# Four output units, two norms and four units behind them, in halves of 256 tokens

## The chip, the cores and the metric

The kernel runs on one core of one Trainium2 chip. The metric is the device time of one execution in microseconds (us), as the median of several. Engines are called as in the profile: PE (TensorE), ACT (ScalarE), DVE (VectorE), POOL (GpSimd), SP (SyncE, which here only issues DMAs).

## The reference

Two transformer blocks follow each other on 512 tokens of width 1024. The change lies at the end of the second block, between its attention and its second feed-forward net, whose first matmuls it also touches:

```python
y = g_na * (o_na.reshape(B, T, -1) @ w_o_na) + g_mla * (o_mla.reshape(B, T, -1) @ w_o_mla)
y = y @ w_out                                       # the second output projection
x = _residual(x, y, g[3], m[5], 1.0)                # x + gate * rmsnorm(y) * gain
h = _modnorm(x, g[4], m[6], m[7])                   # rmsnorm(x) * gain * (1 + scale) + shift
x = _residual(x, _swiglu(h, ffn2_w1, ffn2_w3, ffn2_w2), g[5], m[8], HALF_STEP)
```

Both norms go over the 1024 features of a token, so each waits for the whole row of its input.

## The kernel before, in words

Activations lie transposed: partition = feature, X has 8 tiles of 128 features x 512 tokens. Every matrix is cut into **units** of 1024 x 128 (512 KB) that stream through four slots. A unit's way is always the same: SP's DMA into RAW (`refill`, L433) once `units_done` says that the slot's last unit is through; ACT rounds it to the high part WHI (`convert`, L553); POOL writes the low part WLO = RAW - WHI (`lows`, L455, four instructions of 256 columns), **in the place of RAW**; PE multiplies. Three products (high x low, high x high, low x high) make one exact fp32 product, so a unit on 512 tokens is 24 matmuls. A slot is free for its next DMA only when the last matmul of the unit that it holds has run. All orders are written out by hand, one program for each engine with semaphores.

The stretch of interest, on each engine:

- **PE.** The eight units of the projection, `w_out2` (0 and 1 as a pair, then one after the other, L2343 and L2347, banks m % 4). Then 9 idle matmuls (`spin`, L2424; an fp32 matmul leaves two records), which only keep the engine at work, the ones-matmul that sums the squares of y over the features (`sum_of`, L2433), 14 more idle ones, eight ones-matmuls for the squares of X (L3231), 15 idle ones. Then the four first units of the net, `ffn2` + 0 to 3: 0 and 1 as a `pair`, tile by tile as the normed input arrives (L2368, L2369, L2373), 2 and 3 each whole. Their last matmuls are far apart in time: units 0 and 1 first, 2 then, 3 last. Then `net`: `first_down` (L2853), which multiplies by units `ffn2` + 4 and 5 and needs the weights of + 4, both halves of the gated product (`_l`), and then `seven` for each pair of units.
- **DVE.** For each unit of the projection it copies the product to YO (L2247) and adds ACT's square to the sum (L1376). `post` (L1796 to L1802) scales the eight tiles by the norm's factor and gain, adding the odd ones to X; POOL adds the even ones (`even_tiles`, L469). Then it scales X tile by tile into PSUM (L2264) and writes the low parts HLO (L2258). Three sums for the net follow (L2269 to L2272), `rest_of_sums` with the low parts TLO (L1886), and the copies of `first_down`'s products to Y (L1866) ahead of the first pair's sums (L1941).
- **ACT.** `project` rounds a unit and squares a tile of YO, turn about; `factor` makes Ln and Exp of the sum (L584, L588); L1298 squares X; L1302 and L1303 write HHI and HRAW. `net` begins with `convert` of `ffn2` + 3, the SiLU (L1061), `convert` of + 4 and of + 5, the round of the gated product (L1064) and three rounds THI (L1014).
- **POOL.** `lows` through `ffn2` + 2, the even tiles, then `lows` of + 3, 4 and 5.

Of the kernel before, what the change touches and what calls it, by code (L numbers as in the profile page):

```python
# [22 lines left out]
ALU = mybir.AluOpType  # L23
# [87 lines left out]
for _name, _n in _vec:  # L111
# [43 lines left out]
def build(nc, t):  # L155
    with ExitStack() as ctx:
# [83 lines left out]
        (SQ2, RS2, TN2), _ = region(r_at, ("SQ2", [P, 2, N2], F32), ("RS2", [P, N2], F32), ("TN2", [P, 2, N2], F32))  # L240
# [48 lines left out]
        (YO,), _ = region(g_at, ("YO", [P, KD, S], F32))  # L289
# [157 lines left out]
        def _(pool):  # L447
# [94 lines left out]
        def _(act):  # L542
# [749 lines left out]
            project("yo", "w_out2", "p3", SQ2, YO)  # L1292
            factor("p3", 6)
            for k in range(KD):
                act.wait_ge(*tile_at("p3", k))
                if k >= 2:
                    act.wait_ge(*norm_at("a4", "ms", k - 1))
                nc.scalar.activation(SQ2[:, k % 2, 0:S], X[:, k], ACT.Square).then_inc(s("norm_sq"), 1)  # L1298
            factor("a4", 4, n=KD)
            for k in range(KD):  # L1300
                act.wait_ge(*norm_at("a4", "t", k + 1))
                nc.scalar.activation(HHI[:, k, 0:S], ps[:, (5, 7)[k % 2]], ACT.Identity, bias=mod[:, 6 * KD + k, 0:1]).then_inc(s("norm_hi"), 1)  # L1302
                nc.scalar.activation(HRAW[:, k, 0:S], ps[:, (5, 7)[k % 2]], ACT.Identity, bias=mod[:, 6 * KD + k, 0:1]).then_inc(of_strassen("raw"), 1)  # L1303
# [30 lines left out]
        def _(dve):  # L1334
# [909 lines left out]
            clear(TN2[:, 1, 0:S])  # L2244
            for m in range(KD):
                wait_unit(UNIT["w_out2"] + m)
                V.tensor_copy(YO[:, m], ps[:, m % 4]).then_inc(s("yo"), 1)  # L2247
                add_square("p3", TN2[:, 1, 0:S], SQ2, m, m)
            dve.wait_ge(s("yo"), KD + 4)
            post("p3", lambda k: YO[:, k], cf(6), (5, 7), lambda j: TN2[:, j % 2, 0:S])  # L2250
            dve.wait_ge(*norm_at("p3", "x", KD // 2))
            dve.wait_ge(*norm_at("p3", "px", KD // 2))
            z = NETS[1]

            def last_low(k):
# [73 lines left out]
        def _(pe):  # L2329
# [811 lines left out]
            def latent_values(b):  # L3141
# [8 lines left out]
                mm.then_inc(*((s("mv_ready"), 1) if b < 5 else (units_done, 1)))  # L3150
# [78 lines left out]
            for k in range(KD):  # L3229
# [198 lines left out]
```

## Time and profile before

| | |
|---|---|
| median of 3 runs | 2281.15 us (2280.82 to 2284.95) |
| the profiled execution | 2280.16 us, its span 2278.3 us |
| granted PE clock over the span | 0.998 |
| PE busy | 2218.7 us, 97% |
| the projection's last unit is through; idle matmuls begin | 1892.8 us |
| first matmul of `ffn2` | 1912.05 us |
| first matmul of `first_down` | 1935.58 us |

Times of rows are us from the span's start. A matmul's printed duration is longer than the distance to the next one, since they are pipelined; what a stretch costs is read from starts. "<-" names what ended an idle time.

### The profile page before, as it was taken

What the parts mean: (1) busy time and instruction counts of PE and PEld (TensorE: products, weight loads), DVE (VectorE), ACT (ScalarE), POOL (GpSimd) and SP (SyncE); (2) the same over time, 40 slices, a digit from 0 to 9 for tenths busy, and PEclk for the clock granted to TensorE, in tenths of its full rate; (3) what the DMA queues carried; (4) which work ended last, traced back from release to release, by engine and by line L of the source; (5) the groups of instructions that cost most, each with busy time, mean ns of one, the idle gap of its engine ahead of it and who ended that gap; (6) DMA issues with size and microseconds to landing.
All of it is one profiled execution on the core that took longest, in us unless ns stands there. A gap on an engine that the chain in (4) does not pass through costs nothing.

```text
span 2278.3 us, 34847 instructions
## 1 busy us (share of the span) xinstructions
PE 2218.7 (97%) x12540; PEld 1920.9 (84%) x12540; DVE 1312.9 (58%) x2104; ACT 959.0 (42%) x1490; POOL 1296.7 (57%) x1440
## 2 busy tenths in 40 slices
PE   7999999999999999999999999999989999999997
PEld 6778787678888879999999989877777887999997
DVE  4525632598878778454554655234247546877666
ACT  3354644444233454332332343255546535444443
POOL 3434465199988766554644634333346164887775
PEclk9999999999999999999999999999999999999999
DMA  4322142355555542222212222222230021333232
GB/s 157 104 81 84 56 133 90 111 175 198 198 188 199 186 148 74 66 65 74 75 58 73 75 74 72 75 88 81 67 105 29 20 102 60 98 101 104 95 110 75
DMA packets 67952, 229.27 MB, mean 101 GB/s; under 512 B 7264, under 2 KB 12640, under 8 KB 67680
## 3 DMA queue, kind: packets, MB, share of 16 engines
q1 hardware_dynamic: 50944, 176.67, 23.1%
q10 hardware_dynamic: 16864, 50.60, 6.7%
q8 instruction: 100, 1.64, 0.3%
q14 instruction: 44, 0.36, 0.1%
HBM read 224.36 MB, written 2.10 MB: 99 GB/s over the span
## 4 chain that ended last, share of the span: by engine, by line
PE 81%; DVE 8%; issue 5%; ACT 3%; POOL 3%; DMA 0%; ACTq 0%; POOLq 0%; DVEq 0%; SPq 0%
PE ps L2343 19%; PE ps L2853 11%; PE ps L2347 10%; PE ps L2912 7%; PE ps L2908 7%; PE ps L2909 7%; PE ps L3062 4%; PE ps L2399 3%; POOL WLO L455 2%; PE ps L2354 1%; PE ps L3004 1%; PE ps L3182 1%; PE ps L3033 1%; PE ps L3047 1%; PE ps L3200 1%
## 5 line engine op out<-in xcount | busy, mean ns | idle before, releaser
L455 POOL TENSOR_TENSOR WLO<-RAW,WHI 128x256 fp32r<-128x256 f32 x996 | 865.2, 904 | 708.6 <-ACT WHI L553 708.0
L553 ACT ACTIVATE WHI<-RAW 128x1024 fp32r<-128x1024 f32 x249 | 260.6, 1056 | 275.2 <-DMA RAW<-in_stream_dram 266.6
L474 POOL TENSOR_TENSOR WLO<-RAW,WHI 128x256 fp32r<-128x256 f32 x240 | 235.5, 1002 | 196.4 <-DVE SRAW L1941 77.7
L2343 PE MATMUL ps<-HLO,WHI 128*128 128x512 f32 (+2 forms) x848 | 306.6, 378 | 0.0
L2343 PE MATMUL ps<-HHI,WHI 128*128 128x512 f32 (+2 forms) x848 | 300.5, 371 | 0.0
L2347 PE MATMUL ps<-HHI,WLO 128*128 128x512 f32 (+2 forms) x848 | 192.5, 371 | 0.3 <-POOL WLO L455 0.3
L2343 PEld LDWEIGHTS ps<-HLO,WHI 128*128 128x128 f32 (+1 forms) x848 | 154.7, 188 | 32.4 <-issue 4.3
L2343 PEld LDWEIGHTS ps<-HHI,WHI 128*128 128x128 f32 (+1 forms) x848 | 154.9, 188 | 30.4 <-issue 2.6
L2347 PEld LDWEIGHTS ps<-HHI,WLO 128*128 128x128 f32 (+1 forms) x848 | 149.3, 188 | 28.3 <-POOL WLO L455 0.5
L2853 PE MATMUL ps<-GLO,WHI 128*128 128x384 f32 (+1 forms) x480 | 143.7, 353 | 1.3 <-POOL WLO L455 1.1
L2853 PE MATMUL ps<-GHI,WHI 128*128 128x384 f32 (+1 forms) x480 | 143.5, 353 | 0.0
L2853 PE MATMUL ps<-GHI,WLO 128*128 128x384 f32 (+1 forms) x480 | 143.5, 352 | 0.0
L2908 PE MATMUL ps<-HLO,WHI 128*128 128x384 f32 (+1 forms) x480 | 140.3, 308 | 0.0
L2909 PE MATMUL ps<-HHI,WHI 128*128 128x384 f32 (+1 forms) x480 | 140.3, 308 | 0.0
L1644 DVE SCALAR_TENSOR_TENSOR ADA<-ADA,CB 128x1024 f32<-128x1024 f32 x72 | 107.6, 1495 | 7.6 <-DVE DOT L1644 2.3
L1869 DVE TENSOR_TENSOR Y<-Y,ps 128x768 f32<-128x768 f32 (+1 forms) x72 | 58.9, 818 | 88.5 <-PE ps L2853 88.0
L1644 DVE SCALAR_TENSOR_TENSOR DOT<-ADA,CB 128x1024 f32<-128x1024 f32 x72 | 105.1, 1459 | 5.5 <-issue 5.1
L1031 ACT ACTIVATE SHI<-SRAW 128x512 fp32r<-128x512 f32 x120 | 75.7, 631 | 73.2 <-DVE SRAW L1956 53.8
L1026 ACT ACTIVATE WHI<-RAW 128x1024 fp32r<-128x1024 f32 x80 | 63.8, 838 | 89.9 <-DMA RAW<-in_stream_dram 89.9
L2853 PEld LDWEIGHTS ps<-GLO,WHI 128*128 128x128 f32 x480 | 87.7, 188 | 8.2 <-POOL WLO L455 1.6
L2909 PE MATMUL ps<-THI,SHI 128*128 128x384 f32 (+1 forms) x320 | 93.6, 308 | 0.0
L2908 PE MATMUL ps<-TLO,SHI 128*128 128x384 f32 (+1 forms) x320 | 93.6, 308 | 0.0
(508 smaller groups left out, 5333.9 us busy)
## 6 DMA issues: line engine op xcount, KB each, us to landing
RAW<-in_stream_dram SPq DMA_DIRECT2D x329, 512.0 KB, 3.3
ADA<-in_ada_dram ACTq DMA_DIRECT2D x72, 512.0 KB, 4.0
BM<-in_bias_dram ACTq DMA_DIRECT2D x8, 448.0 KB, 3.9
DECAY<-in_decay_dram ACTq DMA_DIRECT2D x4, 512.0 KB, 3.7
C<-in_ctx_dram ACTq DMA_DIRECT2D x2, 1024.0 KB, 5.5
out_dram<-X SPq DMA_DIRECT2D x16, 128.0 KB, 1.8
X<-in_x_dram SPq DMA_DIRECT2D x2, 512.0 KB, 5.9
X<-in_x_dram ACTq DMA_DIRECT2D x2, 512.0 KB, 6.9
```

The lines of the kernel that those rows point to most:

```text
L455: op = nc.gpsimd.tensor_tensor(WLO[:, slot(u), k:k + 2], RAW[:, slot(u), k:k + 2], WHI[:, slot(u), k:k + 2].bitcast(F32), ALU.subtract)
L474: op = nc.gpsimd.tensor_tensor(WLO[:, j, k:k + 2], RAW[:, j, k:k + 2], WHI[:, j, k:k + 2].bitcast(F32), ALU.subtract)
L553: nc.scalar.activation(WHI[:, j], RAW[:, j], ACT.Copy).then_inc(unit_hi, 1)
L1031: nc.scalar.activation(out, x, ACT.Copy).then_inc(of_strassen("hi"), 1)
L1644: V.scalar_tensor_tensor(out, w, 1.0, CB[:, v], ALU.mult, ALU.mult, accum_out=mod[:, bass.ds(4 * i + a0, 1), v]).then_inc(s("ada_used"), 1)
L2343: nc.tensor.matmul(out, high[k], x[:, k, tok], start=(k == 0 and n == 0), stop=False)
L2347: mm = nc.tensor.matmul(out, low[k], hi[:, k, tok], start=False, stop=(k == kt - 1))
L2853: mm = nc.tensor.matmul(ps[:, bank, 0:n], w[:, j, k0 + k], x[:, k, n0:n0 + n], start=(first and k == ks[0] and i == 0), stop=(final and k ...
L2908: nc.tensor.matmul(product(z, p, n), high[:, k], x_lo[:, k], start=(k == 0 and not more), stop=False, skip_group_check=more)
L2909: nc.tensor.matmul(product(z, p, n), high[:, k], x_hi[:, k], start=False, stop=False, skip_group_check=more)
L2912: mm = nc.tensor.matmul(product(z, p, n), low[:, k], x_hi[:, k], start=False, stop=(k == 3), skip_group_check=more)
L3062: mm = nc.tensor.matmul(ps[:, 7], w, x[:, k, x_tok], start=(k == 0 and n == 0), stop=(k == KD - 1 and n == 2))
```

## The change

The projection's units 4 to 7, both norms and units `ffn2` + 0 to 3 work on 256 tokens at a time, and the norms' element work takes two tiles (2 x 256) in one instruction. The first half of the tokens is normed while PE does the second half of the projection. ACT takes over the copy to YO and puts the gain on it; the gain of the second norm also goes to ACT's bias instruction, so DVE multiplies by the factor alone, into SBUF. All idle matmuls here are gone. The order on PE, ACT and DVE, and on POOL, in the diff's own lines (helpers of one line each, semaphore tables and buffer addresses left out):

```diff
 # PE
-            for m in range(2, KD):
+            for m in range(2, 4):
+                unit(UNIT["w_out2"] + m, 0, [(ps[:, m], x_tok)], hi=HHI, lo=HLO)
...
+            def half_tiles(first, last, h):
+                for b in range(first, last):
+                    wait_weights(UNIT["ffn2"] + b)
+                for j in range(4):
+                    pe.wait_ge(*norm_at("w2", "hi", 8 * h + 2 * j + 2))
+                    for k in (2 * j, 2 * j + 1):
+                        for b in range(first, last):
+                            u, out = slot(UNIT["ffn2"] + b), ps[:, 2 * b, half_of(h)]
+                            nc.tensor.matmul(out, WHI[:, u, k], HHI[:, k, half_of(h)], start=(k == 0), stop=False)
+                            nc.tensor.matmul(out, WLO[:, u, k], HHI[:, k, half_of(h)], start=False, stop=False)
+                    pe.wait_ge(*norm_at("w2", "lo", 4 * h + j + 1))
+                    for b in range(first, last):
+                        for k in (2 * j, 2 * j + 1):
+                            mm = nc.tensor.matmul(ps[:, 2 * b, half_of(h)], WHI[:, slot(UNIT["ffn2"] + b), k], HLO[:, k, half_of(h)],
+                                                  start=False, stop=(k == KD - 1))
+                        if h and j == 3:
+                            mm.then_inc(units_done, 1)
+            for m in range(4, KD):
                 pe.wait_ge(s("yo"), m + 1)
-                unit(UNIT["w_out2"] + m, 0, [(ps[:, m % 4], x_tok)], hi=HHI, lo=HLO)
-            sum_of("p3", TN2[:, 1, 0:S], 6, wait=9, idle=4)
-            spin(4, 14)
-
-            for k in range(KD):
-                pe.wait_ge(*norm_at("a4", "sq", k + 1))
-                nc.tensor.matmul(ps[:, 4], const[:, ONES], SQ2[:, k % 2, 0:S], start=(k == 0), stop=(k == KD - 1)).then_inc(s("norm_ms"), 1)
-            spin(1, 15)
+                out_half(m, 0).then_inc(s("part_ready"), 1)
+            out_half(4, 1)
+            p3_total(0)
+            for m in range(5, KD):
+                out_half(m, 1)
+            a4_total(0)
+            p3_total(1)
+            pe.wait_ge(s("yo"), 16)
+            half_tiles(0, 2, 0)
+            half_tiles(2, 4, 0)
+            a4_total(1)
+            half_tiles(0, 4, 1)
...
-            u = UNIT["ffn2"]
-            pair(u, 0, [[(ps[:, 0], x_tok)], [(ps[:, 2], x_tok)]], HHI, HLO, lambda k: (norm_at("a4", "hi", k + 1), norm_at("a4", "lo", k + 1)))
-            unit(u + 2, 0, [(ps[:, 4], x_tok)], hi=HHI, lo=HLO)
-            unit(u + 3, 0, [(ps[:, 6], x_tok)], hi=HHI, lo=HLO)
 # ACT
+            def out_rows(m, h=None):
...
+                nc.scalar.activation(SQ2[:, m % 2, cols], x, ACT.Square).then_inc(s("norm_sq"), 1)
+                nc.scalar.activation(YO[:, m, cols], x, ACT.Identity, scale=coef[:, 6, m:m + 1]).then_inc(s("yo"), 1)
+            def modulated(h, j):
+                act.wait_ge(*norm_at("w2", "t", 4 * h + j + 1))
+                for b in range(2):
+                    k = 2 * j + b
+                    for dst, landed in ((HHI, s("norm_hi")), (HRAW, of_strassen("raw"))):
+                        nc.scalar.activation(dst[:, k, half_of(h)], Z2[:, j % 2, b], ACT.Identity, bias=mod[:, 6 * KD + k, 0:1],
+                                             scale=coef[:, 7, k:k + 1]).then_inc(landed, 1)
...
+            for m in range(4, KD):
+                out_rows(m, 0)
+            out_rows(4, 1)
+            half_root(0)
+            out_rows(5, 1)
+            convert(UNIT["ffn2"])
+            for j in range(4):
+                pair_square(0, j)
+            out_rows(6, 1)
+            convert(UNIT["ffn2"] + 1)
+            out_rows(7, 1)
+            half_root(1)
+            half_root(2)
+            modulated(0, 0)
+            convert(UNIT["ffn2"] + 2)
+            modulated(0, 1)
+            modulated(0, 2)
+            convert(UNIT["ffn2"] + 3)
+            modulated(0, 3)
+            for j in range(4):
+                pair_square(1, j)
+            half_root(3)
+            for j in range(4):
+                modulated(1, j)
 # DVE
+            add_row(4, 1)
+            gained(0, 0)
+            gained(0, 1)
+            to_x(0, 1)
+            gained(0, 2)
+            gained(0, 3)
+            add_row(5, 1)
+            to_x(0, 3)
+            for j in range(1, 4):
+                add_pair(0, j)
+            add_row(6, 1)
+            add_row(7, 1)
+            scaled_pair(0, 0)
+            scaled_pair(0, 1)
+            for j in range(4):
+                low_pair(0, j)
+                if j < 2:
+                    scaled_pair(0, j + 2)
+                gained(1, j)
+                to_x(1, j)
 # POOL
-            lows(UNIT["o"] + 1, UNIT["ffn2"] + AHEAD)
-            even_tiles("p3", lambda j: TN2[:, j % 2, 0:S])
-            lows(UNIT["ffn2"] + AHEAD, UNIT["ffn2"] + 6)
+            lows(UNIT["o"] + 1, UNIT["ffn2"])
+            for j in (0, 2):
+                x, y = X[:, 2 * j:2 * j + 2, half_of(0)], YO[:, 2 * j:2 * j + 2, half_of(0)]
+                pool.wait_ge(*norm_at("w2", "p", j + 1))
+                nc.gpsimd.tensor_tensor(x, x, y, ALU.add).then_inc(s("norm_px"), 1)
+            lows(UNIT["ffn2"], UNIT["ffn2"] + 6)
```

The helpers: `out_half(m, h)` is a unit on half h in banks 0 to 3 (h = 0) or 4 to 7 (h = 1), and only h = 1 counts it as done; `p3_total` and `a4_total` are the ones-matmuls of the first and second norm; `half_root` is Ln and Exp on 256 columns; `pair_square` squares two tiles of X; `gained` multiplies two tiles of YO by the factor; `to_x` adds them to X; `add_pair` sums squares; `scaled_pair` multiplies two tiles of X by the factor; `low_pair` writes HLO for two tiles. The second half's `add_pair`, `scaled_pair` and `low_pair` follow on DVE as in the first.

## Rows read from the trace of the kernel before

**Rows 1.** The page: busy time of the engines, and the chain's shares.

```profile
PE 2218.7 (97%) x12540; PEld 1920.9 (84%) x12540; DVE 1312.9 (58%) x2104; ACT 959.0 (42%) x1490; POOL 1296.7 (57%) x1440
...
PE 81%; DVE 8%; issue 5%; ACT 3%; POOL 3%; DMA 0%; ACTq 0%; POOLq 0%; DVEq 0%; SPq 0%
```

**Rows 2.** Waits of PE, 1912 to 1950 and 1946 to 2250: total, times, longest.

```profile
PE ps L2853 <- POOL WLO L455: 1.1, 1, 1.1
...
PE ps L2912 <- POOL WLO L474: 1.8, 5, 0.5
```

**Rows 3.** Timeline of PE around the norms: start, duration, engine, line, operation, count.

```profile
1892.79 2.17 PE L2424 MATMUL ps<-const 128*128 128x128 f32 x18
1895.46 1.12 PE L2433 MATMUL ps<-TN,const 128*128 128x512 f32 x2 [0.51 <-DVE TN L1376]
1900.83 8.12 PE L3231 MATMUL ps<-SQ,const 128*128 128x512 f32 x16 [1.11 <-ACT SQ L1298]
1912.05 0.48 PE L2368 MATMUL ps<-HHI,WHI 128*128 128x512 f32 x1
...
1935.58 0.50 PE L2853 MATMUL ps<-GLO,WHI 128*128 128x512 f32 x1 [1.13 <-POOL WLO L455]
...
1946.60 0.28 PE L2908 MATMUL ps<-HLO,WHI 128*128 128x256 f32 x1
```

**Rows 4.** Timeline of PE: last product of a 512-token unit, twice; of 256-token products.

```profile
1880.08 1.98 PE L2347 MATMUL ps<-HHI,WLO 128*128 128x512 f32 x8
...
1885.52 1.98 PE L2347 MATMUL ps<-HHI,WLO 128*128 128x512 f32 x8
...
2250.82 0.64 PE L2347 MATMUL ps<-GHI,WLO 128*128 128x256 f32 x4
...
2252.26 0.64 PE L2347 MATMUL ps<-GHI,WLO 128*128 128x256 f32 x4
```

**Rows 5.** Timeline of ACT: Ln and Exp of a factor on 256 columns.

```profile
2259.41 0.45 ACT L1309 ACTIVATE ps<-ps,small 128x256 f32<-128x256 f32 x1
2259.89 0.37 ACT L1311 ACTIVATE ps<-ps 128x256 f32<-128x256 f32 x1
```

**Rows 6.** Timelines of POOL: lows alone, an addition of 512 columns, lows beside DVE.

```profile
1881.11 2.82 POOL L455 TENSOR_TENSOR WLO<-RAW,WHI 128x256 fp32r<-128x256 f32 x4 [2.42 <-ACT WHI L553]
...
1898.83 1.28 POOL L469 TENSOR_TENSOR X<-X,TN 128x512 f32<-128x512 f32 x1 [3.97 <-DVE TN L1796]
...
1922.82 16.92 POOL L455 TENSOR_TENSOR WLO<-RAW,WHI 128x256 fp32r<-128x256 f32 x12 [16.57 <-ACT WHI L553]
```

**Rows 7.** Timeline of DVE: 512 and 1024 columns from SBUF, alone and beside POOL.

```profile
1912.48 0.69 DVE L2258 TENSOR_TENSOR HLO<-HRAW,HHI 128x512 fp32r<-128x512 f32 x1 [0.67 <-ACT HRAW L1303]
...
1922.43 1.22 DVE L2269 TENSOR_TENSOR TRAW<-HRAW 128x1024 f32<-128x1024 f32 x1
...
1929.98 4.95 DVE L1886 TENSOR_TENSOR TLO<-TRAW,THI 128x1024 fp32r<-128x1024 f32 x3
```

**Rows 8.** A refill: SP's issue of two DMAs, and ACT's rounding of the first.

```profile
1923.51 1.30 SPq L433 DMA_DIRECT2D RAW<-in_stream_dram  x2
...
1927.42 1.06 ACT L553 ACTIVATE WHI<-RAW 128x1024 fp32r<-128x1024 f32 x1 [2.77 <-DMA RAW<-in_stream_dram]
```

**Rows 9.** Timeline of PE at both ends of the kernel, and a stretch's granted clock (PEclk).

```profile
12.71 2.08 PE L2424 MATMUL ps<-const 128*128 128x128 f32 x8 [12.71 <-DMA vec<-in_vec_dram]
...
16.29 3.38 PE L2424 MATMUL ps<-const 128*128 128x128 f32 x18
...
2258.68 0.70 PE L3237 MATMUL ps<-TN,const 128*128 128x256 f32 x2 [1.46 <-DVE TN L1376]
...
2263.52 2.17 PE L2424 MATMUL ps<-const 128*128 128x128 f32 x18
2268.53 1.22 PE L3237 MATMUL ps<-TN,const 128*128 128x256 f32 x2 [2.84 <-DVE TN L2287]
...
2268.00:2270.00 2.00, 1.22 (x2) 0.50 (x2) 1.29 (x3) 0.21 (x1) 0.19 (x1) 0.55 0.39 132
```

More of the change, by code:

```diff
@@ L1291, in _ @@
             nc.scalar.preload_act_table_set("natural_log_exp_and_others")
-            project("yo", "w_out2", "p3", SQ2, YO)
-            factor("p3", 6)
-            for k in range(KD):
[L1295 to L1303, printed above, removed]
+            def out_rows(m, h=None):
+                cols = half_of(h) if h is not None else slice(0, S)
+                if h == 0:
+                    act.wait_ge(s("part_ready"), 5 + m - 3)
+                else:
+                    wait_unit(UNIT["w_out2"] + m)
+                if h != 1 and m >= 2:
+                    act.wait_ge(*p3_sum(m - 2, 0))
+                elif h == 1 and m >= 6:
+                    act.wait_ge(*p3_sum(m - 2, 1))
+                x = ps[:, m % 4] if h is None else ps[:, m % 4 + 4 * h, 0:M]
+                nc.scalar.activation(SQ2[:, m % 2, cols], x, ACT.Square).then_inc(s("norm_sq"), 1)
+                nc.scalar.activation(YO[:, m, cols], x, ACT.Identity, scale=coef[:, 6, m:m + 1]).then_inc(s("yo"), 1)
@@ new lines, in half_root, with pair_square @@
+            def half_root(n):
+                x = ps[:, 1 + 2 * (n % 2), 0:M]
+                act.wait_ge(*norm_at("w2", "ms", n + 1))
+                nc.scalar.activation(x, x, ACT.Ln, scale=1.0 / D, bias=eps).then_inc(s("norm_ln"), 1)
+                act.wait_ge(*norm_at("w2", "ln", n + 1))
+                nc.scalar.activation(RS2[:, n], x, ACT.Exp, scale=-0.5).then_inc(s("norm_rs"), 1)
+            def pair_square(h, j):
+                act.wait_ge(*summed(h, j))
+                if j == 0 and h:
+                    act.wait_ge(*norm_at("w2", "ms", 2))
+                elif j == 3:
+                    act.wait_ge(*norm_at("w2", "acc", A4_ADD[h]))
+                elif j and h:
+                    act.wait_ge(*norm_at("w2", "acc", A4_ADD[0] + (2 if j == 1 else 1)))
+                nc.scalar.activation(SQXP[:, (j - 1) % 2] if j else ACCX[:], X[:, 2 * j:2 * j + 2, half_of(h)], ACT.Square).then_inc(s("norm_sq"), 1)
@@ new lines, in modulated @@
+            def modulated(h, j):
[5 more added lines that the diff above has]
+                                             scale=coef[:, 7, k:k + 1]).then_inc(landed, 1)
+            for m in range(4):
+                convert(UNIT["w_out2"] + AHEAD + m)
+                out_rows(m)
@@ L2268, in _ @@
+            for j in range(1, 4):
+                add_pair(1, j)
+            dve.wait_ge(*norm_at("w2", "x", 6))
+            dve.wait_ge(*norm_at("w2", "rs", 4))
+            scaled_pair(1, 0)
+            scaled_pair(1, 1)
+            for j in range(4):
+                low_pair(1, j)
+                if j < 2:
+                    scaled_pair(1, j + 2)
             first, second, third = (sums_of(z, TRAW, n) for n in range(3))
@@ L3232, in _, with out_half, p3_total @@
-            spin(1, 15)
+            for m in range(2, 4):
+                unit(UNIT["w_out2"] + m, 0, [(ps[:, m], x_tok)], hi=HHI, lo=HLO)
+            def out_half(m, h):
+                return unit(UNIT["w_out2"] + m, 0, [(ps[:, m % 4 + 4 * h, 0:M], half_of(h))], hi=HHI, lo=HLO, last=(h == 1))
+            def p3_total(h):
+                pe.wait_ge(*p3_sum(7, h))
+                if h:
+                    pe.wait_ge(*norm_at("w2", "rs", 1))
+                nc.tensor.matmul(ps[:, 1, 0:M], const[:, ONES], ACC2[:, half_of(h)], start=True, stop=True).then_inc(s("norm_ms"), 1)
@@ new lines, in a4_total @@
+            def a4_total(h):
+                pe.wait_ge(*norm_at("w2", "acc", A4_ADD[h] + 2))
+                pe.wait_ge(s("yo"), 12)
+                for b in range(2):
+                    mm = nc.tensor.matmul(ps[:, 3, 0:M], const[:, ONES], ACCX[:, b], start=(b == 0), stop=(b == 1))
+                mm.then_inc(s("norm_ms"), 1)
+            def half_tiles(first, last, h):
+                for b in range(first, last):
+                    wait_weights(UNIT["ffn2"] + b)
+                for j in range(4):
+                    pe.wait_ge(*norm_at("w2", "hi", 8 * h + 2 * j + 2))
[11 more added lines that the diff above has]
+                            mm.then_inc(units_done, 1)
```

95 lines of the change are left out of this document (68 added, 27 removed).

## The prediction

> **What bounds the kernel now.** The page first: PE is busy 97% of the span and carries 81% of the chain that ended last [rows 1]. So an edit pays only where it takes idle time, idle matmuls or stalls out of PE's program, and costs whatever it lets PE wait. PE's waits come next. From 1946 to 2250 PE waits 1.8 us in all, in five pieces [rows 2]: what moves the first matmul of `seven`, at 1946.60 [rows 3], moves the end by the same amount. Ahead of that lie two places. Between the projection's last unit (1892.79) and the first matmul of `ffn2` (1912.05) PE does 19.3 us of idle matmuls and ones-matmuls while ACT and DVE norm [rows 3]: that is what the change goes for. And at 1935.58 `first_down` has waited 1.1 us for POOL's low part of unit `ffn2` + 4 [rows 2, 3]. This second wait shows that the weights' way is already as late as PE there, though units 0 and 1 were through at 1923.5 and 10.9 us of PE work on units 2 and 3 covered it.
>
> **The parts, step by step** (times on the scale of the profiled span).
>
> (1) *Halves of units.* A 512-token unit takes 1885.52 - 1880.08 = 5.44 us for 24 matmuls; 12 matmuls on 256 tokens take 1.44 us [rows 4], so half a unit takes 2.88 and a unit in halves 5.76. Eight units in halves cost 8 x 0.32 = 2.6 us more PE time, nothing hides it. From 1871.05 (unit 4 starts, four units of 5.44 ahead of 1892.8): 8 x 2.88 + 0.46 for the first ones-matmul (the distance from 2258.68 to the next is below 0.70 [rows 9]) ends at 1894.6, where whole units ended at 1892.8.
>
> (2) *First norm, half 0.* It now lies beside the projection. Half 0 of unit 7 ends 1882.6, its ones-matmul behind unit 4's second half at 1886.0; Ln and Exp take 0.45 + 0.37 with 256 columns [rows 5], so DVE begins `gained` at 1887.3. Beside POOL a DVE instruction on two SBUF operands is slower and POOL too: POOL's 256 columns take 2.82 / 4 = 0.71 us alone and 16.92 / 12 = 1.41 beside a busy DVE [rows 6]; DVE's 1024 columns take 1.22 alone and 1.65 beside POOL, its 512 columns 0.69 alone [rows 7]. Bounds: no slowing at all, and POOL at half its rate. I take 0.68 of its rate for DVE and 0.55 for POOL, nearer the rows with both busy, because all new DVE instructions here have two SBUF operands, where `post` read PSUM. POOL's two additions of 512 columns (1.28 alone [rows 6]) then end at 1893.0, X is whole, and only now do POOL's `lows` of `ffn2` + 0 start: they stand behind both additions on its queue.
>
> (3) *PE waits for it.* `lows` of + 0 end at 1897.7 and of + 1 at 1902.0, since ACT rounds + 1 behind four squares of X and `out_rows(6, 1)`, at 1896.4. The factor for X (sum of squares, 0.95 for two ones-matmuls, 1.9 us of ACT for the two roots, then `scaled_pair`, three bias instructions of 0.36, by the 0.37 of Exp) would be there at 1900.3. So `half_tiles(0, 2, 0)` starts at 1902.0, ten us before 1912.05, but with nothing on PE between 1898 and 1902.
>
> (4) *The first half pass starves.* It is 5.76 us of PE work, fed by DVE in the order low, scaled, gained, to_x: twelve instructions up to the last `low_pair`, at 0.62 to 0.68 us alone and 0.9 to 1.0 beside POOL, which does `lows` of + 2 and + 3 all the time. It ends at 1912.5, 4.7 us lost. `half_tiles(2, 4, 0)` is 5.76 us without a wait: 1918.3.
>
> (5) *Second half's norm.* `a4_total(1)` stands behind that pass on PE though its squares are ready at 1915.4: 0.95, then Ln and Exp 0.82, `scaled_pair` 0.62, three bias instructions 1.08, handing over four times 0.1: PE stands still 3.0 us and `half_tiles(0, 4, 1)` starts at 1922.2. 11.5 us: all four units are through at 1933.7. Before, unit 3 was through at 1934.3. So the 19.3 us of norms under PE's own work have given 0.6 us: 2.6 go to halves, 2.8 to the ones-matmuls of all four sums, 13.8 to the waits of (2) to (5), some 1.6 of them between unit 7 and the ones-matmuls behind it.
>
> (6) *The refill has lost its cover.* Here the change is dear. No slot is free before the last eight matmuls of `half_tiles(0, 4, 1)`, since `units_done` counts there for all four. Units + 4 and + 5 are fetched into slots 0 and 1. Before, the DMA went out at 1923.51 and ACT began to round at 1927.42 [rows 8], 3.9 us; ACT 1.0; POOL 2.8 alone to 5.6 beside DVE [rows 6]. Now the DMA goes out at 1933.5, rounding begins at 1936.9, POOL begins at 1938.0 and ends at 1942.7: `first_down` starts at 1942.8, 7.2 us later than before, after 9.1 us in which PE does nothing. Bounds of this wait: 7.2 with POOL alone, 9.5.
>
> (7) *Behind it.* ACT rounds the first gated product and all three THI behind `convert(+4)`, so DVE's TLO and the second GLO, which lay beside units 2 and 3 before, now lie beside `first_down`: its fifth part waits 1.7 us for GLO and `seven` 0.4 for POOL. `seven` starts at 1955.7 instead of 1946.6: **+9.1 us**. With no slowing between POOL and DVE the same steps give 1948.1, +1.5.
>
> (8) *The clock.* Idle matmuls are gone. At the kernel's start PE's 128-column matmuls take 2.08 / 8 = 0.26 us a record, against 2.17 / 18 = 0.12 later: the clock stood at 1.2 and not 2.4 GHz, and the 18 records from 16.29 still take 3.38 us. Near the end, after 2.84 us of idleness behind a run of idle matmuls, the ones-matmul takes 1.22 instead of 0.70 us and the granted clock of the stretch is 0.55 [rows 9]. So idle stretches of 4.0, 3.0 and 9.1 us can each drop it, and what follows runs at half speed until it rises. In the first place DVE is the limit anyway (0), in the third 1.7 us are covered by the wait for GLO. Bounds: 0, and 3 us in the second place and 1.3 in the third (6 us at half speed, as from 12.71 until some way into the records of 16.29 [rows 9]). I take 1.5 in all, nearest to one drop partly covered.
>
> The Trainium skill ("TensorE: Matmul & The Clock Gate", Part 1) says that half rate is the default, which activity lifts and an idle stretch brings back. By that rule both the second and the third place pay, as an estimate, about 3 us together in place of 1.5.
>
> **Sum.** 9.1 + 1.5 = 10.6 on the execution's own 2280.16; the median of the runs is 1.0 above it, so 2281.15 + 10.6 = 2291.8, said as 2291.5.
>
> **The rivals.** A difference under 0.2%, 4.6 us, is about what measuring this kernel can't tell from no change.
>
> - *Forecast, 0.62:* as summed, 2287 to 2295.
> - *POOL and DVE hardly disturb each other, 0.16.* Then + 1.5 by step (7), to 4.5 with the clock: 2282.6 to 2285.7. For it: POOL's rows alone at 0.71 are many, and DVE is idle at times in the new stretch. Against it: 1.41 us for twelve instructions in a row just there [rows 6].
> - *They exclude each other wholly, 0.10.* While one has two SBUF operands the other waits, both at half rate. `half_tiles(0, 4, 1)` then starts at 1927.3, `first_down` at 1948.3, `seven` at 1963.9: +17, 2298. Against it: 1.65 of DVE's 1.22 beside POOL's 1.41 of 0.71 adds up to 1.24 of one engine's rate, not to 1 [rows 6, 7]. The Trainium skill states this one ("SBUF — State Buffer", "SBUF: two separate sides"): VectorE and GpSimd share a port pair by an exclusive lock, also where VectorE has two SBUF inputs and GpSimd reads SBUF. By it the rival holds; the trace agrees only in that both slow down.
> - *The stalls close and it is faster, 0.04.* `first_down` can start 8 to 9 us after the units are through, whatever comes before. PE's own work from 1871.05 to there is 23.0 + 0.5 + 1.0 + 0.5 + 11.5 + 1.0 + 11.5 = 49.0. With 1.5 us of stalls they are through at 1921.5, `first_down` starts at 1930: -5.6, 2275.5. It decides at `units_done`: under 3 us of stalls for over 0.2% faster, where step (5) alone has 3.0.
> - *The clock stays low over long stretches, 0.08:* half speed through `half_tiles(0, 4, 1)` and `first_down` costs up to 6 us more, 2297.
>
> The range, 2284.5 to 2298, takes in the forecast, most of the second rival and the two dear ones. Faster 0.04; same 0.12, nearly all of it the second rival; slower 0.84.
>
> **What would show it.** PE's idle stretch ahead of `first_down` should be 7 to 10 us long, released by POOL's `lows` and behind them by the DMA; the four last units through between 1929 and 1936; four refills issued one behind the other there; about 3 us of idleness behind `a4_total(1)`; POOL's `lows` of + 0 to + 3 at over 1 us an instruction; granted clock below 1 somewhere between 1898 and 1950; from `seven` on the same rows as before, later by the sum. A wait of `first_down` under 5 us, or units through before 1926, would prove me wrong.

## The result and the profile after

The changed kernel takes **2296.79 us** (median of 4 runs, 2294.06 to 2297.35) against 2282.54 (2280.82 to 2284.95) of the kernel before beside it: ratio **1.0062**, 95% interval 1.005 to 1.0074. It is slower, within the range and 5.3 us above the number forecast. The profiled execution, the fastest of the four, took 2294.06 us, its span 2292.3, 14.0 above before; granted PE clock 0.992. Of the 5.3 us, 1.4 are the higher median of before here (2281.15 when the forecast was made); the other 3.9 are the forecast's.

The page's busy time of PE, and PE's waits from 1870 to 1990 us (releaser, total, times, longest), against [rows 1, 2]:

```profile
PE 2215.2 (97%) x12650; PEld 1928.1 (84%) x12650; DVE 1320.4 (58%) x2108; ACT 970.0 (42%) x1526; POOL 1293.0 (56%) x1438
```

```profile
PE ps L3004 <- POOL WLO L484: 9.1, 1, 9.1
PE ps L3405 <- ACT HHI L1365: 6.5, 3, 3.4
PE ps L3410 <- DVE HLO L2375: 2.8, 3, 1.3
PE ps L3393 <- DVE ACCX L2362: 2.8, 1, 2.8
```

PE's busy time barely fell: idle matmuls left, but halves and matmuls at half clock came in. 21.2 us of waits (the four totals together) stand in a stretch of 89. PE's timeline there, against [rows 3]:

```profile
1898.55 2.07 PE L3393 MATMUL ps<-ACCX,const 128*128 128x256 f32 x4 [2.76 <-DVE ACCX L2362]
...
1904.11 0.35 PE L3405 MATMUL ps<-HHI,WHI 128*128 128x256 f32 x1 [2.63 <-ACT HHI L1365]
...
1913.37 0.74 PE L3410 MATMUL ps<-HLO,WHI 128*128 128x256 f32 x4 [1.31 <-DVE HLO L2375]
...
1916.26 0.74 PE L3410 MATMUL ps<-HLO,WHI 128*128 128x256 f32 x4 [1.19 <-DVE HLO L2375]
...
1922.59 1.02 PE L3393 MATMUL ps<-ACCX,const 128*128 128x256 f32 x4
...
1927.06 0.35 PE L3405 MATMUL ps<-HHI,WHI 128*128 128x256 f32 x1 [3.44 <-ACT HHI L1365]
...
1947.89 0.80 PE L3004 MATMUL ps<-GLO,WHI 128*128 128x512 f32 x1 [9.09 <-POOL WLO L484]
1948.49 0.63 PE L3004 MATMUL ps<-GHI,WHI 128*128 128x512 f32 x1
1948.92 0.63 PE L3004 MATMUL ps<-GHI,WLO 128*128 128x512 f32 x1
...
1961.10 0.28 PE L3059 MATMUL ps<-HLO,WHI 128*128 128x256 f32 x1
```

The first norm is under the projection as meant: the pass on half 0 starts at 1904.11. The gain is lost in these four groups of waits, the dearest ahead of `first_down`. How that one comes about is in the timelines of SP, ACT and POOL, against [rows 8]:

```profile
1938.26 2.47 SPq L462 DMA_DIRECT2D RAW<-in_stream_dram  x4
...
1941.53 1.06 ACT L585 ACTIVATE WHI<-RAW 128x1024 fp32r<-128x1024 f32 x1 [2.80 <-DMA RAW<-in_stream_dram]
...
1942.66 9.38 POOL L484 TENSOR_TENSOR WLO<-RAW,WHI 128x256 fp32r<-128x256 f32 x8 [27.61 <-ACT WHI L585]
```

All four refills go out at 1938.26, when PE has nothing left to do. POOL had been idle for 27.6 us. The same stretch by the granted clock (window, length, PE busy and its records, PEclk, DMA share, GB/s):

```profile
1898.00:1901.40 3.40, 2.85 (x6) 0.50 0.18 72
...
1904.80:1911.60 6.80, 6.08 (x27) 0.50 0.00 1
1911.60:1942.40 30.80, 21.27 (x168) 1.00 0.10 30
1942.40:1952.60 10.20, 4.71 (x11) 0.50 0.33 119
```

**How the runs below are compared.** Identical code ahead of the stretch ends up to 5.9 us apart in the profiled executions (unit 4 of the projection starts at 1869.07 in one, at 1874.99 in another). So all are measured from that start, t4, up to the first matmul of `first_down` and of `seven`. These three columns are one profiled execution for each kernel; how far the stretch of one kernel varies between executions wasn't measured, beyond what the medians say.

| | median us | ratio to before (95%) | t4 | `first_down` - t4 | `seven` - t4 |
|---|---|---|---|---|---|
| before | 2282.54 | | 1871.02 | 64.56 | 75.58 |
| after | 2296.79 | 1.0062 (1.005 to 1.0074) | 1872.18 | 75.71 | 88.92 |
| late_release | 2292.32 | 1.0049 (1.0032 to 1.0066) | 1874.12 | 73.16 | 86.11 |
| split_last | 2291.29 | 1.0048 (1.0031 to 1.0064) | 1869.07 | 72.08 | 84.72 |
| with_idle | 2293.67 | 1.0059 (1.0042 to 1.0076) | 1870.77 | 74.79 | 86.76 |
| sum_early | 2290.54 | 1.0042 (1.0028 to 1.0057) | 1871.83 | 72.89 | 86.06 |
| psum_factor | 2292.16 | 1.0048 (1.0031 to 1.0065) | 1874.74 | 72.75 | 86.06 |
| pair_round | 2297.90 | 1.0074 (1.0057 to 1.0091) | 1874.06 | 78.41 | 90.78 |
| before_no_idle | 2283.92 | 1.0009 (1.0 to 1.0019) | 1874.99 | 66.10 | 76.98 |
| all_mends | 2283.42 | 1.0008 (0.9998 to 1.0017) | 1871.12 | 65.37 | 78.02 |
| norm_first | 2285.80 | 1.0016 (1.0007 to 1.0025) | 1872.79 | 68.06 | 80.04 |
| unit3_whole | 2283.20 | 1.0006 (0.9997 to 1.0015) | 1871.31 | 65.95 | 77.92 |
| norm_first_whole | 2285.26 | 1.0016 (1.0007 to 1.0025) | 1872.38 | 68.29 | 80.25 |

Each ratio is against runs of before on the same chip (their medians 2280.8 to 2282.5). The medians' distances to their own before are, in the order of the table from after on, 14.3, 11.5, 10.5, 12.9, 9.8, 10.9, 16.6, 2.6, 2.1, 4.6, 2.0 and 4.0 us; the stretch gives the same within 1.8 us. So the change costs 88.92 - 75.58 = **13.3 us in the stretch**; 1.2 more lie ahead of t4 in code that the change leaves alone, and 0.5 come back behind `seven`: 14.0.

### The profile page after: what moved, and what is told of

Its sections match the earlier page's. It is cut to its first block, busy times and chain, and to the rows that moved or that the text cites. A ratio compares the mean times of both kernels' runs of the same rounds, so it can differ in the third digit from the quotient of the medians.

```text
span 2292.3 us, 35086 instructions
## 1 busy us (share of the span) xinstructions
PE 2215.2 (97%) x12650; PEld 1928.1 (84%) x12650; DVE 1320.4 (58%) x2108; ACT 970.0 (42%) x1526; POOL 1293.0 (56%) x1438
## 4 chain that ended last, share of the span: by engine, by line
PE 55%; POOL 22%; issue 17%; DVE 4%; ACT 1%; POOLq 0%; DMA 0%; ACTq 0%; DVEq 0%; SPq 0%
POOL WLO L484 21%; PE ps L3004 12%; PE ps L2494 7%; PE ps L3063 7%; PE ps L3060 7%; PE ps L3059 7%; PE ps L3213 4%; PE ps L2498 3%; PE ps L2550 2%; PE ps L3155 1%; PE ps L3333 1%; PE ps L3184 1%; PE ps L3198 1%; PE ps L3351 1%; POOL WLO L503 1%
## 5 line engine op out<-in xcount | busy, mean ns | idle before, releaser
L3004 PEld LDWEIGHTS ps<-GHI,WLO 128*128 128x128 f32 x480 | 88.3, 189 | 6.5
L3004 PEld LDWEIGHTS ps<-GHI,WHI 128*128 128x128 f32 x480 | 88.4, 189 | 6.2
```

The costliest lines, as they stand in the source:

```text
L3004: mm = nc.tensor.matmul(ps[:, bank, 0:n], w[:, j, k0 + k], x[:, k, n0:n0 + n], start=(first and k == ks[0] and i == 0), stop=(final and k ...
```

## The experiments

**late_release: only the slots, in the kernel before.** The four units run as before, but all four slots count as free together, behind the last.

```diff
-            pair(u, 0, ..., HHI, HLO, ...)
-            unit(u + 2, 0, [(ps[:, 4], x_tok)], hi=HHI, lo=HLO)
-            unit(u + 3, 0, [(ps[:, 6], x_tok)], hi=HHI, lo=HLO)
+            pair(u, 0, ..., HHI, HLO, ..., count=False)
+            unit(u + 2, 0, [(ps[:, 4], x_tok)], hi=HHI, lo=HLO, last=False)
+            unit(u + 3, 0, [(ps[:, 6], x_tok)], hi=HHI, lo=HLO, last=False).then_inc(units_done, 4)
```

> The kernel before, in which the four first units of the second net count as done only together, behind the last matmul of unit 3; nothing else differs. If the refill's lost cover is the cost (my theory), first_down waits 9 us as in the changed kernel (9.09 there, 1.1 before), starts near 1943 to 1945 instead of 1935.6, and the kernel is 7 to 10 us slower than before: near 2291. If the wait in the changed kernel comes from the norms' lateness or from POOL and DVE slowing each other, and the release matters little because POOL was already late in the kernel before, first_down waits under 4 us here and the time is within 3 us of before.

Timelines of SP, ACT, POOL and PE:

```profile
1937.64 2.47 SPq L433 DMA_DIRECT2D RAW<-in_stream_dram  x4
...
1940.90 1.06 ACT L553 ACTIVATE WHI<-RAW 128x1024 fp32r<-128x1024 f32 x1 [2.79 <-DMA RAW<-in_stream_dram]
...
1942.04 8.26 POOL L455 TENSOR_TENSOR WLO<-RAW,WHI 128x256 fp32r<-128x256 f32 x7 [10.70 <-ACT WHI L553]
...
1947.28 0.79 PE L2853 MATMUL ps<-GLO,WHI 128*128 128x512 f32 x1 [9.81 <-POOL WLO L455]
```

The same chain, and a wait of 9.8 us, as expected; the time is above the 7 to 10 us expected. This edit alone costs 86.11 - 75.58 = **10.5 us of the stretch** (13.3 after the change), and the median 11.5 of 14.3, without halves, norms or new work for POOL and DVE. 8.6 of the 10.5 lie ahead of `first_down`. The other 1.9 lie between it and `seven`, where the granted clock is 0.50 from 1941.6 to 1951.2, behind the wait.

**split_last: only the slots, in the kernel after.** The last pass goes unit pair by unit pair, so slots 0 and 1 are free half-way.

```diff
-            half_tiles(0, 4, 1)
+            half_tiles(0, 2, 1)
+            half_tiles(2, 4, 1)
```

> The changed kernel with the second half's pass over four units cut into units 0 and 1, then 2 and 3, so that two slots come free before the last two units. Theory of the cover: 5.8 us of PE work now lie behind the release, but the first of the two passes is fed by ACT at 0.49 us an instruction, 1.97 us for a pair of tiles against 1.44 on PE, and ends some 2.5 us late; the first DMA goes out 2.5 to 4 us earlier, first_down starts 2.5 to 4 us earlier, and its idle wait falls from 9.1 to 3 or 4 us. Time 2.5 to 4 us below the changed kernel, 2293 to 2294.5. Rival (norms or POOL set the start of first_down): no change, or 2 us slower by the starved pass.

PE's timeline and SP's:

```profile
1931.40 6.67 SPq L462 DMA_DIRECT2D RAW<-in_stream_dram  x4
...
1941.15 0.50 PE L3004 MATMUL ps<-GLO,WHI 128*128 128x512 f32 x1 [3.92 <-POOL WLO L484]
```

and a window of its last pass by the granted clock:

```profile
1921.70:1928.50 6.80, 5.38 (x25) 0.50 0.00 0
```

The wait falls from 9.1 to 3.9 us, by 5.2, and the stretch by 4.2. The rest is the clock, which fell elsewhere in this execution: the last pass, part of it at half clock, takes 14.1 us where the changed kernel took 11.7; against that, 0.8 us come ahead of it, where the ones-matmuls took 1.13 instead of 2.07 us, and 0.6 behind, between `first_down` and `seven`.

**with_idle: the clock.** The after kernel with idle matmuls in its four gaps.

```diff
             for m in range(5, KD):
                 out_half(m, 1)
+            pe.wait_ge(s("yo"), 12)
+            spin(0, 10)
             a4_total(0)
             p3_total(1)
             pe.wait_ge(s("yo"), 16)
+            spin(5, 10)
             half_tiles(0, 2, 0)
             half_tiles(2, 4, 0)
             a4_total(1)
+            spin(5, 12)
             half_tiles(0, 4, 1)
+            spin(5, 34)
```

> The changed kernel with idle matmuls in the four places where PE stands still. Theory of the clock: the clock stays at 2.4 GHz from 1895 to 1955; the ones-matmuls of 2.07 and 1.06 us fall to 1.0 and 0.6 us, first_down's first matmuls come 0.23 us apart instead of 0.42; as the wait for weights stays 9 us and the GLO wait then shows, 2 to 4 us faster than the changed kernel: 2293 to 2295. If the clock costs nothing that other waits don't cover: same within 1 us. If the idle matmuls themselves delay what follows: slower.

Windows of PE (columns as above), and PE's wait for the low parts:

```profile
1896.00:1904.00 8.00, 6.60 (x44) 1.00 0.14 55
1904.00:1912.00 8.00, 3.75 (x27) 1.00 0.01 2
...
1942.00:1953.00 11.00, 8.99 (x49) 1.00 0.10 40
```

```profile
PE ps L3410 <- DVE HLO L2375: 4.7, 3, 2.3
```

The clock stays whole and the stretch is 2.2 us shorter, 0.9 ahead of `first_down` and 1.2 between it and `seven` (12.0 us instead of 13.2; a wait of 0.6 for GLO shows there now, which half clock had covered). 0.8 of the 0.9 are there when the first pass starts, since the ones-matmuls took 1.13 us instead of 2.07. In the pass itself the full clock buys nothing: PE only waits longer for DVE (4.7 us instead of 2.8). Between the last unit and `first_down` still lie 9.1 us, now filled with idle matmuls and a wait of 1.4. The median is 12.9 us above its own before, 1.4 less than that of the changed kernel.

**sum_early: the second half's sum ahead of unit 3 of half 0.**

```diff
-            half_tiles(2, 4, 0)
+            half_tiles(2, 3, 0)
             a4_total(1)
+            half_tiles(3, 4, 0)
```

> The changed kernel with the second half's sum of squares taken between unit 2's and unit 3's first halves instead of behind both. The chain Ln, Exp, scale, bias then lies beside 2.9 us of PE work: PE's wait of 3.4 us ahead of the last pass falls to about 0.6, and everything behind comes 2.8 us earlier: 2294 (2.8 below the changed kernel). If the start of first_down is set by POOL or DVE and not by the last pass, the end doesn't move.

PE's timeline at the last pass and at `first_down`:

```profile
1923.99 0.35 PE L3405 MATMUL ps<-HHI,WHI 128*128 128x256 f32 x1 [0.58 <-ACT HHI L1365]
...
1944.72 0.80 PE L3004 MATMUL ps<-GLO,WHI 128*128 128x512 f32 x1 [8.99 <-POOL WLO L484]
```

The 3.44 us behind the sum shrink to 0.58, and `seven` comes 2.9 earlier, all of the gain. The wait of 9 us stays whole: it starts earlier, and that is all. The two are additive, as a wait for a refill that is issued only when the work is over must be.

**psum_factor: POOL against DVE.** Exp leaves the factor in PSUM, and DVE's `gained` and `scaled_pair` read it there: one operand of two leaves SBUF. So that both halves' factors can stay there, each half gets columns of its own in the bank; nothing else changes.

```diff
-                nc.scalar.activation(RS2[:, n], x, ACT.Exp, scale=-0.5).then_inc(s("norm_rs"), 1)
+                nc.scalar.activation(x, x, ACT.Exp, scale=-0.5).then_inc(s("norm_rs"), 1)
...
-                V.tensor_tensor(y, y, RS2[:, 2 * h].unsqueeze(1).to_broadcast([P, 2, M]), ALU.mult).then_inc(s("norm_p"), 1)
+                V.tensor_tensor(y, y, ps[:, 1, half_of(h)].unsqueeze(1).to_broadcast([P, 2, M]), ALU.mult).then_inc(s("norm_p"), 1)
```

> The changed kernel with the norm factors left in PSUM (RS2 isn't used), so that gained and scaled_pair, 16 instructions of 512 columns, have one SBUF operand in place of two. If POOL and DVE slow each other only where DVE reads two SBUF operands (as I charged it), these instructions fall from 1.22 to about 0.75 us beside POOL, POOL's lows of units 1 to 3 from 1.1 to 0.9 an instruction, and the first half pass, now 14.2 us, ends 2 to 3 us earlier: 2 to 3 us faster than the changed kernel, 2292 to 2293. If the operands' place doesn't matter and any DVE work slows POOL: no change in the durations and in the time.

First the after kernel's timeline of DVE in the first pass, and POOL's beside it:

```profile
1905.80 1.22 DVE L2349 TENSOR_TENSOR YO<-YO,RS 128x512 f32<-128x512 f32 x1
...
1908.08 1.22 DVE L2375 TENSOR_TENSOR HLO<-HRAW,HHI 128x512 fp32r<-128x512 f32 x1
1909.22 1.21 DVE L2368 TENSOR_TENSOR Z<-X,RS 128x512 f32<-128x512 f32 x1
1910.36 0.68 DVE L2349 TENSOR_TENSOR YO<-YO,RS 128x512 f32<-128x512 f32 x1
...
1905.48 4.40 POOL L484 TENSOR_TENSOR WLO<-RAW,WHI 128x256 fp32r<-128x256 f32 x4 [3.84 <-ACT WHI L585]
1910.37 4.68 POOL L484 TENSOR_TENSOR WLO<-RAW,WHI 128x256 fp32r<-128x256 f32 x4 [0.48 <-ACT WHI L585]
```

and the same of psum_factor:

```profile
1909.71 0.67 DVE L2368 TENSOR_TENSOR Z<-X,ps 128x512 f32<-128x512 f32 x1
1910.31 0.67 DVE L2349 TENSOR_TENSOR YO<-YO,ps 128x512 f32<-128x512 f32 x1
...
1911.62 1.23 DVE L2375 TENSOR_TENSOR HLO<-HRAW,HHI 128x512 fp32r<-128x512 f32 x1
...
1906.66 3.72 POOL L484 TENSOR_TENSOR WLO<-RAW,WHI 128x256 fp32r<-128x256 f32 x4 [3.21 <-ACT WHI L585]
```

With a PSUM operand DVE's instruction takes 0.67 us while POOL is at work. With both in SBUF it takes 0.68 where it begins while POOL stands idle (as at 1910.36, in POOL's gap of 0.48 us), and 1.1 to 1.2 where POOL is at work. POOL's four go from 4.40 to 3.72. So DVE and POOL do hinder each other where both work in SBUF, as the prediction had it. `seven` comes 2.9 us earlier. Not all of that is sharing: about 0.6 lie between the ones-matmuls and the start of the first pass, and those matmuls took 1.31 instead of 2.07 us, since the clock fell only at 1901.2, near their end.

**pair_round: fewer bias instructions on ACT.** HHI is rounded from HRAW by one Copy of two tiles, in place of two bias instructions; DVE's `low_pair` waits for HHI instead of HRAW.

```diff
-                    for dst, landed in ((HHI, s("norm_hi")), (HRAW, of_strassen("raw"))):
-                        nc.scalar.activation(dst[:, k, half_of(h)], Z2[:, j % 2, b], ACT.Identity, ...)
+                    nc.scalar.activation(HRAW[:, k, half_of(h)], Z2[:, j % 2, b], ACT.Identity, ...)
+                act.wait_ge(*strassen_at(NETS[1], "raw", 8 * h + 2 * j + 2))
+                nc.scalar.activation(HHI[:, 2 * j:2 * j + 2, half_of(h)], HRAW[:, 2 * j:2 * j + 2, half_of(h)], ACT.Copy).then_inc(s("norm_hi"), 2)
```

> The changed kernel with ACT writing HRAW by two bias instructions and HHI by one rounding copy of both tiles, three instructions of some 1.5 us for a pair in place of four of 1.97. If ACT, which I costed too low (0.36 against 0.49 measured), feeds the first half pass: it shortens by 1.5 to 2 us. If DVE's row of low, scaled, gained and to_x feeds it (as the prediction has it): under 1 us, since low_pair comes no earlier. The wait ahead of first_down stays at 9 us in both.

A window in its last pass:

```profile
1928.10:1934.90 6.80, 6.03 (x28) 0.50 0.00 0
```

A miss: 1.9 us more, not less. The last pass takes 14.4 us instead of 11.7, at half clock for 6.8 us; whether that drop comes from the edit isn't known. It starts 54.8 us behind t4, where it was 54.9: fewer instructions on ACT did not bring PE's work forward, which speaks for the expectation's other branch, in which DVE feeds the first half pass. That HHI, which PE wants first, now stands behind both HRAW may also have cost (the wait for the first HHI is 3.0 us instead of 2.6); this wasn't tested alone.

**before_no_idle: what idle matmuls are worth before.** The kernel before without its 9, 14 and 15 idle matmuls.

```diff
-            sum_of("p3", TN2[:, 1, 0:S], 6, wait=9, idle=4)
-            spin(4, 14)
+            sum_of("p3", TN2[:, 1, 0:S], 6)
...
-            spin(1, 15)
```

> The kernel before without its 38 idle matmuls around the two sums. Clock theory: PE then stands still 2.6 us, 3 us and 3.3 us among few ones-matmuls, the clock falls to 1.2 GHz in one or two pieces of the stretch from 1893 to 1912, the first tiles of the pair run at half speed behind it, and the kernel is 1.5 to 3 us slower than before. If the idle matmuls were worth nothing: same within 0.5 us, clock 1.0.

```profile
1904.72 9.48 PE L3230 MATMUL ps<-SQ,const 128*128 128x512 f32 x16 [4.22 <-ACT SQ L1298]
```

The eight ones-matmuls on PE's timeline take 9.48 instead of 8.12 us [rows 3], with a granted clock of 0.50 from 1901.6 to 1908.0, and the stretch 1.4 more. The median is 2.6 us above before, the interval's lower end at 1.0. Removing the idle matmuls is no saving; here it is a small loss.

**all_mends: split_last, sum_early, psum_factor and pair_round together**, with 8 idle matmuls in each of three gaps, the last ahead of `first_down`.

> The changed kernel with all of it: split last pass, early sum, factors in PSUM, pairwise rounding, idle matmuls in the shorter gaps. The single gains against the changed kernel's seven-start of 1961.1 (before 1946.6) were 2.9 for the early sum and 5.2 for the earlier release; with 2 for PSUM and 1 for the clock seven starts near 1950 and the kernel takes 2284 to 2286, still 1 to 4 us above before, since 2.6 us of halves and 2 us of ones-matmuls stay. If the refill's cover was the whole cost: at or below before, 2280 or less.

PE's timeline:

```profile
1919.96 0.36 PE L3406 MATMUL ps<-HHI,WHI 128*128 128x256 f32 x1 [0.79 <-ACT HHI L1367]
...
1936.49 0.50 PE L3005 MATMUL ps<-GLO,WHI 128*128 128x512 f32 x1 [2.26 <-POOL WLO L484]
```

10.9 of the 13.3 us are gone; the mends that gained alone (4.2, 2.2, 2.9, 2.9) sum to 12.2. It is equal to the kernel before within the interval, and no better. Of the 2.4 us left in the stretch, 0.8 lie ahead of `first_down`, behind a gap of 4.2 us from the last unit (idle matmuls and the wait of 2.26), and 1.6 between it and `seven` (12.65 us against 11.02), with the clock at 0.50 from 1938.0 to 1941.2.

**norm_first, unit3_whole, norm_first_whole: getting below before.** In all_mends, DVE does the second half's norm ahead of the first half's last low parts (norm_first); unit `ffn2` + 3 runs whole behind the halves, as cover for the refill (unit3_whole); both. The idle matmuls differ too: norm_first has 14 instead of 8 ahead of `first_down`; the other two have 8 more behind the early sum and 4 instead of 8 ahead of `first_down`. In norm_first ACT's squares of the second half move forward with DVE's work.

```diff
 # unit3_whole, PE
-            half_tiles(3, 4, 0)
             half_tiles(0, 2, 1)
-            half_tiles(2, 4, 1)
+            half_tiles(2, 3, 1)
+            unit(UNIT["ffn2"] + 3, 0, [(ps[:, 6], x_tok)], hi=HHI, lo=HLO)
 # norm_first, DVE
+            for j in range(2):
+                low_pair(0, j)
+                scaled_pair(0, j + 2)
+                gained(1, j + 2)
+                to_x(1, j + 2)
+            add_pair(1, 1)
+            low_pair(0, 2)
+            add_pair(1, 2)
+            add_pair(1, 3)
+            low_pair(0, 3)
```

> all_mends with DVE and ACT doing the second half's first norm and squares ahead of the first half's last low parts. In all_mends DVE is busy without a break from 1901.5 to 1915.1, when the squares are summed, and PE begins the last two passes at 1919.96. If DVE's order is what holds the last passes, they begin 1 to 2.5 us earlier and the kernel takes 1 to 2 us less than all_mends (0.1% below before to 0.05% above). If PE's first pass, which now gets its low parts later, holds them instead: no gain.

> all_mends with unit 3 done whole, last, behind both halves of units 0, 1 and 2, so that 8.3 us of PE work in place of 5.8 cover the refill. In all_mends first_down starts 10.4 us after the first slot is free, of which 4.2 show. Theory of the cover: PE loses up to 2.6 us ahead of the last passes, where unit 3's first half was, and gets 2.6 back ahead of first_down: within 1 us of all_mends. If the cover didn't matter beyond 5.8 us: 2 us slower than all_mends.

> Both edits of norm_first and unit3_whole. The second norm comes earlier, which fills the gap that unit 3's first half left, and the refill has 8.3 us of cover: 2 to 3.5 us below all_mends, 2280 to 2281.5, at before or 0.05% below it. If the first pass on PE holds back the last ones: as all_mends.

PE's timeline of norm_first:

```profile
1913.14 1.22 PE L3418 MATMUL ps<-HLO,WHI 128*128 128x256 f32 x4 [2.35 <-DVE HLO L2378]
```

norm_first is a miss, 2.0 us worse: PE's first pass waits for the low parts that were moved back, and its last passes start 51.3 us behind t4 instead of 48.8. unit3_whole, as expected, comes out within 1 us of all_mends. It cuts the gap between the last unit and `first_down` from 4.2 to 1.5 us (the wait in it from 2.26 to 0.39), yet `seven` comes as late: the last passes start 48.8 us behind t4 in both, so the time that unit 3's first half filled ahead of them has only become idle matmuls and a longer wait (1.87 us instead of 0.79). Both together are a miss as well: 80.25 us, where all_mends has 78.02.

## Why the prediction was right, and what was mis-sized

The sign, the place and the mechanism held: all slots are released together, the refill has no cover, `first_down` waits. late_release shows it alone, split_last shows it from the other side. Of the signs listed, two missed: the four units are through at 1938.7, outside 1929 to 1936, and POOL's `lows` of + 1 take 0.76 us an instruction, not over 1.

- **Steps (1), (2):** as costed. The eight half units end 23.4 us behind t4; POOL's additions end at 1893.66, forecast 1893.0 + 1.2 for the later t4.
- **Step (3)** failed in its releaser. The pass starts at 1902.9 on the forecast's scale (1.2 taken off for t4), not 1902.0, and for ACT's HHI, not for POOL, whose `lows` of + 1 were through at 1901.65 of the trace. The term too small was the factor's chain, forecast at 1900.3 and there 2.7 us later. Two of its parts are in rows: the ones-matmuls for X ran at half clock (2.07 us of records where they take 1.02 at 1922.59), and ACT's bias instructions start 0.5 apart, not 0.36, and take 0.6, so the third ends 1.7 us behind the first one's start where 1.1 was forecast. The rest lies ahead of the ones-matmuls for X, for which PE waited 2.8 us on DVE's sums of squares. Exp on 256 columns [rows 5] was the wrong neighbour for an instruction with a scale and a bias per partition. ACT's timeline after:

```profile
1902.38 0.60 ACT L1365 ACTIVATE HHI<-Z,mod,coef 128x256 fp32r<-128x256 f32 x1
1902.89 0.59 ACT L1365 ACTIVATE HRAW<-Z,mod,coef 128x256 f32<-128x256 f32 x1
```

- **Step (4)** held in kind, and DVE's rate too: its twelve instructions start at 1904.59 to 1915.52, 0.99 us apart on average, for the 0.9 to 1.0 of the forecast. (The average is partly luck: four took 0.68 us, with POOL idle when they began or just beginning, and eight 1.1 to 1.2.) But the pass took 1904.11 to 1916.84, 12.7 us and not 10.5. The step let DVE begin with the chain at 1900.3, ahead of PE, which was still waiting for POOL; with the chain 2.7 us late DVE began behind PE and had no lead. So the one mis-sized chain makes most of the 3.2 us of steps (3) and (4).
- **Step (5):** a wait of 3.44 where 3.0 stood. The last pass ends 3.8 us later than forecast (3.2, and 0.6 from this step). So "have given 0.6 us" was wrong: through at 66.5 behind t4 against 63.3 before, the halves lose 3.2. The step's list (2.6, 2.8, 13.8) adds up to 19.2, which leaves 0.1 of 19.3; the other 0.5 is that the pair took 11.4 us before, where two units take 10.9.
- **Step (6):** 9.09 us for 9.1. From issue to ACT 3.3 us (3.4 forecast, where the step's own row has 3.9 and no reason is given for less), to POOL 1.1 (1.1), to `first_down` 5.2 (4.8).
- **Step (7)** took the right amount for the wrong reason. `first_down` to `seven` takes 13.2 us where before took 11.0; but no wait for GLO shows. The matmuls start about 0.43 us apart instead of 0.23, at half clock, until 1952.6, and that hides whatever GLO had cost. With the clock whole (with_idle) it still takes 12.0, of which 0.6 is the wait for GLO, not 1.7.
- **Step (8):** 1.5 stood for places two and three. With_idle puts the whole clock at about 2.2 us; it also adds idle matmuls of its own, so that is no pure price. The first place, put at nothing, cost 0.8 by the ones-matmuls; the second, behind `a4_total(1)`, stayed whole in this execution, and fell in split_last and pair_round; the third cost 1.2. The estimate of 3 us, made by the rule of the Trainium skill ("TensorE: Matmul & The Clock Gate", Part 1), is no better borne out in its size; the rule, that idleness brings half rate back, agrees at 1942.4, 3.6 us into the wait.
- The sum was 10.6, of which 9.1 by steps (1) to (7); the stretch shows 13.3. To the 9.1 come 3.9 ahead of `first_down` (steps 3 to 5) and 0.3 behind it (2.2 in place of the 1.9 of step (7)). The 1.5 of step (8) isn't added: what the clock cost lies within these pieces. So steps (3) to (5) were short by 3.9, step (8) was counted on top, and it is partly luck that the sum came out nearer than its steps.

**The rivals.** "Hardly disturb" falls: psum_factor takes 2.9 us off, most of it by sparing DVE the sharing in two of its four kinds of instruction. And even so it stands at 2292.2, not at 2282.6 to 2285.7. "Exclude each other wholly" fits the single instruction: with both operands in SBUF 0.68 us beside an idle POOL and 1.1 to 1.2 beside a busy one, 0.67 with one in PSUM. That agrees with the exclusive lock of the Trainium skill ("SBUF — State Buffer", "SBUF: two separate sides"), which also has an operand in PSUM free DVE of it. But its price fails. From 1905.80 to 1910.36, where both are at work, DVE's instructions start 1.14 us apart and POOL takes 1.10 for 256 columns, against about 0.6 and 0.71 alone: together some 1.2 of one engine's rate, where the rival has 1 and the forecast took 1.23 (0.68 and 0.55). Over the pass POOL also stood idle at times, so DVE averaged 0.99, and the 17 us didn't come. "The stalls close" stays out of reach: all_mends closed most and came out level.

What stays open: why the clock falls behind a given wait in one execution and not in another, what part of with_idle's 2.2 us is the clock alone, and what share of the 13.3 us each single mend would have with the clock held whole. A version with the refills' order changed on POOL wasn't tried.

## What to carry to other kernels

Before units that share a weight ring are interleaved or cut in halves, write down when each slot's last reader runs, and what PE does until the refill is back: DMA 3.3, rounding 1.1 and low part 5.2 us here, 9.6 in all. What is won upstream can be lost again if the interleaved pass frees every slot at its end; a last pass cut so that the slots needed first are free first took the wait from 9.1 to 3.9 us here. And a wait that idle matmuls filled is not saved by taking them out: where operands come late the engine only waits, and here a slower clock came behind it (1.4 us more in the stretch).

## What the runs showed that I had not expected

The granted clock also falls in code that the change leaves alone, and not in every execution. Windows of all engines at 826 us (length, busy time of PE, PEld, DVE, ACT, POOL each with records, PEclk, DMA share, GB/s), first after and then before:

```profile
826.00:830.00 4.00, 4.00 (x13) 3.12 (x12) 3.21 (x5) 1.29 (x3) 3.35 (x4) 0.57 0.42 168
```

```profile
826.00:830.00 4.00, 4.00 (x19) 3.32 (x18) 3.33 (x5) 1.29 (x3) 3.23 (x3) 1.00 0.49 190
```

The same code does 13 records in one and 19 in the other. PE is busy in the whole window, but an idle wait lies just ahead of it, and it does so in both; PE's timelines, after and before:

```profile
825.33 0.47 PE L2505 MATMUL ps<-GLO,WHI 128*128 128x512 f32 x1 [1.81 <-POOL WLO L484]
```

```profile
825.44 0.47 PE L2354 MATMUL ps<-GLO,WHI 128*128 128x512 f32 x1 [1.78 <-POOL WLO L455]
```

After, the clock fell to 0.50 at 826.2 for 3.4 us; before, it stayed whole behind the same wait. The same holds at 1679.4, behind a wait of 3.46 us (3.45 before, where nothing fell). Such drops shift everything behind them and are part of why t4 differs by up to 5.9 us: the two kept executions without one ahead of t4 have it at 1869.07 and 1871.02, the four with about 10 us at half clock at 1872.79 to 1874.99. A single profile can't tell an edit's effect below that. Relative starts within a stretch can do better, but the clock also falls at different places within the stretch, so differences of 1 or 2 us there need its windows beside them.
